# The first unit of an output projection, computed tile by tile beside the tail of the last HGRN head, with its residual reloaded in three parts

## What is computed

```
hn = rms_norm(h, mix_norm[0])
proj = hn @ w_in_even[0]
y_a = s5_mixer(...)                      # (T, 512), with its GLU
y_b = hgrn2_mixer(q, f, i, g, ...)       # (T, 512), 4 heads of 128
h = h + concatenate([y_a, y_b]) @ w_out_even[0]
hn = rms_norm(h, mlp_norm[0])
h = h + square(relu(hn @ w_mlp_in[0])) @ w_mlp_out[0]

# one HGRN head: o = recurrence(q, k, v);
# o = o * rsqrt(mean(o*o) + EPS) * head_norm * silu(g)
```

## Time and profile before

| | us |
|---|---|
| median of 3 runs (2578.96 to 2580.57) | 2580.14 |
| the profiled execution, its own time | 2579.56 |
| its span in the trace | 2577.6 |
| PE busy | 2460.5 (95%) |
| DVE busy | 1162.0 (45%) |
| POOL busy | 815.6 (32%) |
| ACT busy | 552.6 (21%) |

### The profile page before, as it was taken

One profiled execution on the slowest core, in us unless ns is written; L12 is line 12 of the kernel. 1 busy time (PEld: TensorE's weight loads), 2 busy tenths in 40 slices (PEclk: granted clock), 3 DMA queues, 4 the chain that ended last, 5 costly groups with the idle time before them and its releaser, 6 DMA issues.

```text
span 2577.6 us, 32642 instructions
## 1 busy us (share of the span) xinstructions
PE 2460.5 (95%) x13054; PEld 1996.1 (77%) x13054; DVE 1162.0 (45%) x1176; ACT 552.6 (21%) x854; POOL 815.6 (32%) x492
## 2 busy tenths in 40 slices
PE   8999957999999999999997999989999999999997
PEld 6887845788888888888885776668888888888885
DVE  6877378332432423325527355652432332424625
ACT  3120255211001010011212145631001001011215
POOL 3433212223333333333232243543333333333321
PEclk9998978999999999999998999999999999999998
DMA  7362431311111111111212111121111111111211
GB/s 209 104 113 82 117 99 35 106 49 49 49 49 49 49 49 47 44 48 49 66 49 90 41 26 57 41 58 41 49 49 49 49 49 49 49 46 46 63 49 65
DMA packets 249159, 159.64 MB, mean 62 GB/s; under 512 B 32132, under 2 KB 236136, under 8 KB 249064
## 3 DMA queue, kind: packets, MB, share of 16 engines
q1 hardware_dynamic: 235528, 139.69, 18.8%
q10 hardware_dynamic: 13552, 18.81, 2.8%
HBM read 131.81 MB, written 25.49 MB: 61 GB/s over the span
## 4 chain that ended last, share of the span: by engine, by line
PE 87%; DVE 8%; ACT 2%; issue 2%; ACTq 1%; DMA 0%; POOL 0%; POOLq 0%; DVEq 0%; SPq 0%
PE ps L612 71%; PE ps L1091 3%; PE ps L763 2%; PE ps L1123 2%; PE ps L1051 1%; DVE hg_queries_keys L1885 1%; PE ps L1064 1%; PE ps L1075 1%; PE ps L784 1%; PE ps L799 1%; PE ps L679 1%; PE ps L988 1%; DVE stage L1543 1%; ACT x_hi L1174 1%; DVE s_state L1613 1%
## 5 line engine op out<-in xcount | busy, mean ns | idle before, releaser
L475 POOL CAST w_hi<-w_raw 128x1024 fp32r<-128x1024 f32 x198 | 211.1, 1066 | 1481.4 <-PE ps L612 1125.1
L612 PE MATMUL ps<-x_hi,w_hi 128*128 128x512 f32 x1600 | 496.4, 392 | 6.5 <-issue 3.2
L612 PE MATMUL ps<-x_lo,w_hi 128*128 128x512 f32 x1600 | 493.5, 390 | 0.0
L612 PE MATMUL ps<-x_hi,w_lo 128*128 128x512 f32 x1600 | 493.1, 389 | 0.0
L477 POOL TENSOR_TENSOR w_lo<-w_raw,w_hi 128x1024 fp32r<-128x1024 f32 x198 | 478.9, 2419 | 15.9
L612 PE MATMUL ps<-mid_hi,w_hi 128*128 128x512 f32 x1216 | 375.8, 390 | 8.7 <-DVE mid_lo L1937 5.8
L612 PE MATMUL ps<-mid_lo,w_hi 128*128 128x512 f32 x1216 | 375.3, 390 | 0.0
L612 PE MATMUL ps<-mid_hi,w_lo 128*128 128x512 f32 x1216 | 375.3, 390 | 0.0
L612 PEld LDWEIGHTS ps<-x_hi,w_hi 128*128 128x128 f32 x1600 | 299.8, 188 | 73.3 <-issue 8.7
L612 PEld LDWEIGHTS ps<-x_lo,w_hi 128*128 128x128 f32 x1600 | 300.9, 188 | 62.8
L612 PEld LDWEIGHTS ps<-x_hi,w_lo 128*128 128x128 f32 x1600 | 300.6, 188 | 62.9
(11 more groups left out here) (290 smaller groups left out, 2453.2 us busy)
## 6 DMA issues: line engine op xcount, KB each, us to landing
w_raw<-w_mlp_in_in SPq DMA_DIRECT2D x64, 512.0 KB, 4.0
w_raw<-w_mlp_out_in SPq DMA_DIRECT2D x64, 512.0 KB, 4.0
w_raw<-w_in_even_in SPq DMA_DIRECT2D x20, 512.0 KB, 4.6
residual_dram<-residual ACTq DMA_DIRECT2D x2, 4096.0 KB, 13.0
w_raw<-w_ple_gate_in SPq DMA_DIRECT2D x16, 512.0 KB, 3.9
fqig_dram<-stage SPq DMA_DIRECT2D x11, 512.0 KB, 3.1
x_tokens<-x_in SPq DMA_DIRECT2D x8, 512.0 KB, 7.3
w_raw<-w_out_even_in SPq DMA_DIRECT2D x8, 512.0 KB, 4.1
```

Of the source, the lines that this page charges most:

```text
L475: pool.tensor_copy(WH[:, b, :], RAW[:, b, :]).then_inc(S["w_hi_done"], 1)
L612: ins = pe.matmul(acc[:, h, :], w[:, k, :], x[:, k0 + k, h * HALF:(h + 1) * HALF], start=(k == 0 and w is wh and x is xh), stop=(k == kts ...
```

## The change

Unit 24 gets banks of its own, 4 and 5 (`OUT_FIRST`), and is computed by `out_first(ks)`, tile by tile. In PE's order k = 0 and 1 stand right behind the eight key transposes of head 3, ahead of `state_steps`; k = 2 to 7 stand behind the last `head_squares`. A tile k of 4 or more waits for that head's `hg_y_low` alone. Units 25 to 31 are as they were: unit 25 goes to ACC[1], and unit 26, into ACC[0], still waits until unit 24 has been read out.

On SP, slabs 24 and 25 are loaded right behind the loads of head 3, when slabs 22 and 23 have been split. The residual comes back in three transfers instead of one: tiles 0 to 1 and 4 to 7 when both sums of squares of head 3 are done (`hg_ss` 8), tiles 2 to 3 when `hg_y_low` is 8. The loop that loads slabs starts at 26.

On DVE the read-out of this projection is `out_residual`, with its 8 tiles written out instead of a loop, since tile 0 reads other banks; it waits for all three transfers. Two later counts of `h_restored` on POOL grow by 32.

```diff
+        OUT_FIRST = PS[:, 4:6, :]
...
                 head_load(hd)
-            sp.wait_ge(S["hg_y_low"], 2 * HEADS)
-            sp.wait_ge(S["h_spilled"], 16)
-            sp.dma_start(H[:, :, :], h_dram.rearrange("(k p) t -> p k t", p=P)).then_inc(S["h_restored"], 16)
-            with sp.Fori(1, 4) as i:
+            for b in range(2):
+                load(b, 24 + b - 1, cols(w, slice((2 + b) * P, (3 + b) * P)))
+
+            def heads_done(tiles):
+                sp.dma_start(H[:, tiles, :], h_dram[tiles.start * P:tiles.stop * P, :].rearrange("(k p) t -> p k t", p=P))\
+                    .then_inc(S["h_restored"], 16)
+
+            sp.wait_ge(S["h_spilled"], 16)
+            sp.wait_ge(S["hg_ss"], 2 * HEADS)
+            heads_done(slice(0, 2))
+            heads_done(slice(4, 8))
+            sp.wait_ge(S["hg_y_low"], 2 * HEADS)
+            heads_done(slice(2, 4))
+            with sp.Fori(2, 4) as i:
...
+            def out_first(ks):
+
+                for k in ks:
+                    pe.wait_ge(S["mid_ready"], 8)
+                    if k >= 4:
+                        pe.wait_ge(S["hg_y_low"], 2 * (k - 3))
+                    for w, x in ((whs[0], XBh), (whs[0], XBl), (wls[0], XBh)):
+                        for h in range(2):
+                            ins = pe.matmul(OUT_FIRST[:, h, :], w[:, k, :], x[:, k, h * HALF:(h + 1) * HALF],
+                                            start=(k == 0 and w is whs[0] and x is XBh), stop=(k == KT - 1 and w is wls[0]))
+                return ins
...
                         if hd and half == 1 and l in (4, 5):
                             head_squares(tail, l - 4)
-
-            pe.wait_ge(S["hg_y_low"], 2 * HEADS)
-            pe.wait_ge(S["mid_ready"], 8)
-            one(22, 24, XB)
+                        if hd == HEADS and half == 1 and l == 0:
+                            pe.wait_ge(S["w_ready"], 23)
+                            pe.wait_ge(S["hg_near_read"], HEADS)
+                            out_first((0, 1))
+
+            out_first(range(2, KT)).then_inc(S["acc_done"], 1)
             one(23, 25, XB)
             run(24, 26, 6, XB)
...
+            def out_residual(u0, norm, gain):
+
+                start_norm()
+                for m in range(KT):
+                    dve.wait_ge(S["acc_done"], u0 + m + 1)
+                    tt(H[:, m, :], flat(ACC[m % 2] if m else OUT_FIRST), H[:, m, :], ALU.add).then_inc(S["acc_free"], 1)
+                    dve.wait_ge(S["acc_free"], free_of(u0)[1] + m)
+                    dve.nop().then_inc(S["h_ready"], 1)
+                    low(norm, m, gain)
+                end_norm()
...
-            dve.wait_ge(S["h_restored"], 16)
-            residual(UNIT["out"], 1, ("mlp", 0), None)
+            dve.wait_ge(S["h_restored"], 48)
+            out_residual(UNIT["out"], 1, ROW["mlp"])
```

More of the change, by code:

```diff
@@ L574, in add_part @@
                 pool.wait_ge(S["part_copied"], 2 * m + 2)
-                pool.wait_ge(S["h_restored"], 32 if m < 4 else 48)
+                pool.wait_ge(S["h_restored"], 64 if m < 4 else 80)
                 pool.tensor_tensor(H[:, m, :], H[:, m, :], PART[:, m, :], ALU.add).then_inc(S["h_part"], 1)
```

## The result

The changed kernel takes 2565.25 us (median of 5 runs, 2565.04 to 2571.07), against 2579.45 us for the kernel before (5 runs): a ratio of 0.995 with a 95% interval of 0.9937 to 0.9964. The forecast was 2569.2 us, with a range from 2567.5 to 2573.2. The direction was right; the measured gain of 14.2 us is larger than the range allowed. In two further measurements the changed kernel had medians of 2566.22 and 2565.69 us, so that its 15 runs have a median of 2565.69 us and a mean of 2566.76; those of the kernel before lie between 2573.01 and 2584.52 us with a median of 2578.80 and a mean of 2578.77 us (76 runs). The gain that stays is 13.1 us by the medians and 12.0 us by the means: three of the 15 runs lie near 2571 us, which the mean counts and the median does not.

What follows compares the result with a forecast made beforehand. PE, busy for 95% of the span, was taken as the bound. Gains of 2.7, 5.8 and 2.34 us made 10.9 us; from the median of 2580.14 us this gave 2569.2 us, range 2567.5 to 2573.2.

Steps and rivals of the forecast that it cites:

- What bounds the kernel, and what unit 24's end is worth: PE bounds the kernel; whatever time unit 24 ends earlier, everything behind it starts earlier, unless another wait takes over.
- Tiles 0 and 1 at 2.73 us in the first hole: 12 matmuls at 2.4 GHz fit PE's 3.27 us gap between head 3's key transposes and state matmuls.
- The rule on transposes: Transposes on PE do not keep the full clock, so tiles 0 and 1 behind them would likelier take 5.1 us.
- The tail, taken as 0: Head 3's state matmuls and outputs together take what they took before: 0, between -0.65 and +3.4 us.
- Tiles 2 to 7, and the low clock of unit 24: 36 matmuls behind the sums of squares fill PE's second hole, 5.8 us, and remove 2.34 us of low clock.
- Residual and slabs: Three-part residual lands at 473.4, margin 2.4 us before unit 26, cost 0; early slabs are a condition for the gain.
- The first rival: Residual transfers served one after another come too late; unit 26 stalls 4.0 us: 2573.2, or 2575.5 us; chance 0.13.
- A little for the runs' own spread: Allowance at the range's lower end, below 11.6 us of gain, giving 2567.5 us.
- the low-clock cases: Rival: tiles 0 and 1 or head 3's outputs run at 1.2 GHz; gain 5.7 to 9 us, 2571 to 2574.4; chance 0.08.

Runs made afterwards that it cites:

- the experiment without the first hole: Changed kernel with all eight tiles of unit 24 behind the sums of squares, none between key transposes and state matmuls: 2569.48 us, ratio 0.9963.
- PE's part alone: Changed kernel with SP as before (one residual transfer, slabs 24 and 25 behind it), PE and DVE as changed: 2575.01 us, ratio 0.9983.

## Why the prediction was wrong

**What bounds the kernel, and what unit 24's end is worth: right.** What is won up to unit 25 arrives at the end. The eight units behind unit 24 take 87.04 us without a gap, and the means of all runs differ by 12.0 us, against 11.7 us in the stretch. A single pair of profiles could not show this, since all that lies behind unit 25 moves by up to 4.5 us.

**Tiles 0 and 1 at 2.73 us in the first hole: right.** They ran from 444.19 to 447.2 at a granted clock of 1.00, and in none of the nine profiles with these tiles behind the key transposes does the clock fall below 1.00 before head 3's sums of squares are done. The rule on transposes that was weighed against it (the Trainium skill, "TensorE: Matmul & The Clock Gate", Part 4) did not decide here.

**The tail, taken as 0: mis-sized, the first step that failed.** Between -0.65 and +3.4 us I took 0. Measured from the key transposes to the squares, the tail takes 10.8 us in the changed kernel and 11.5 to 11.6 us in the three profiles with both holes open, so the term was -0.7 us, the low end. The outputs ran at the full clock. The low clock does reach the first outputs in two profiles in which the first hole is open (the second of the kernel before and the experiment without the first hole), but in none in which it is filled.

**Tiles 2 to 7, and the low clock of unit 24: right in kind, 0.4 us short against the first profile.** I took 10.93 us for a unit from another place in the kernel; here it is 10.88, so unit 24 had taken 13.67 and not 13.27 us. With 10.9 + 0.4 + 0.7 the sum is the 12.05 us of the table. Over the three profiles with both holes open unit 24 takes 13.35 us on average, so most of this 0.4 us was that one execution's.

**Residual and slabs: right.** The last part landed at 470.40, 27.2 us behind the transposes (forecast 473.4 - 445.65 = 27.8), and DVE had read unit 24 by 472.56, 2.5 us before unit 26 needed it; the forecast margin was 2.4. The first rival, transfers served one by one, fell: 4 MB in three parts took 14.35 us from the first issue, one transfer took 14.2. The Trainium skill ("DMA: Bandwidth & Descriptors", Anatomy of one DMA) gives a fixed part of about 2 us for a transfer issued by GpSimd; these were issued by SP. With it on each, served one by one they would have needed some 18 us, an estimate that the trace's 14.35 us does not bear out. That the early slabs are needed was right in kind, but they are a condition for 1.0 us of the gain and not for all of it; with both parts of SP undone unit 26 is 6.6 us late.

**The spread of the runs: the step that put the result outside the range.** "A little for the runs' own spread" below the largest gain of 11.6 us was 1.0 us (2580.14 - 11.6 = 2568.5, range from 2567.5), read off three runs that lay within 1.6 us. The kernel before has a spread of 11.5 us over 76 runs, the changed one 6.7 us over 15, and a single profile carries up to 4 us of it ahead of the change and as much behind. The forecast was also built on the median of those three runs, 1.3 us above the 2578.80 us of all 76.

The result lies 3.95 us under the forecast. Of these, 0.8 us are the change itself (11.7 us in the stretch on average, forecast 10.9), nearly all of it the tail; 1.3 us are the level that was subtracted from; and 0.4 us are that the first five runs of the changed kernel lay under the median of its 15. The remaining 1.4 us are the medians' gain of 13.1 us over the 11.7 us of the traces. By the means only 0.3 us remain, so no run shows a gain outside the stretch. The size of the change was thus nearly right: with the tail at -0.7 us the forecast would have been 2568.5 us, still inside the range. What put the result outside it is the runs' spread. The range has a second slip, which did not matter: its upper end, 2573.2 us, was said to take in the low-clock cases, which reach 2574.4 us.

## What to carry to other kernels

A hole on PE can cost more than its length when the clock falls behind it: here 9.1 us of holes cost 2.9 us on top, and even work that is thrown away won that back. When an accumulation is taken apart to fill holes, list what was hidden behind the old order (the reload of the residual, the next weights), since PE's part alone kept only 4 of 13 us. And before putting a bound on a forecast of half a percent, find out what two profiles of the same kernel differ by; time a change from a marker that it does not touch, and up to one behind it.

## Not expected

The executions of one and the same kernel differ by where in the HGRN stage PE is granted half its clock. The same instructions took 14.42 and 16.73 us, and the start of head 3's key transposes moved over 4.04 us in 13 profiles. Four of them came from one chip (442.59, 444.29, 442.89 and 445.70 us), so it is not a matter of the chip. Nor is it how much low clock there is: from 380 us to the transposes the mean granted clock is 0.90 in the first profile of the kernel before and 0.84 in the second, which is the faster one. What decides where the clock falls is not shown. The shape of this stage is thus one draw for each execution, and comparisons of single profiles across it are worth no more than some 4 us.
